# Borders between the 18 stages of two transformer stacks: sums signalled by quarters, squares by quarters, and a new order on VectorE and ScalarE

## The chip, the cores and the metric

The kernel runs on one core of a Trainium2 chip. The metric is the device time of one execution, in microseconds (us). TensorE does the matrix products, ScalarE (ACT) and VectorE (DVE) everything between them, GpSimd (POOL) a few column operations, and SyncE (SP) only issues the loads of the weight stream.

## The reference, cut to what matters

The program pushes 256 tokens of width 1024 through two stacks. What the change touches is not the layers but what stands between them: residual addition and root mean square normalization.

```python
# first stack, 2 layers ("plain" borders)
x = x + 0.5 * swiglu(rms_norm(x, ffn1_norm[l]), ffn1_w13[l], ffn1_w2[l])
h = rms_norm(x, mix_norm[l])
...                                   # three attentions and gates, merged
x = x + jnp.sum(gates * proj, axis=2) @ w_out[l]
x = x + 0.5 * swiglu(rms_norm(x, ffn2_norm[l]), ffn2_w13[l], ffn2_w2[l])
...
return rms_norm(x, final_norm)
# second stack, 4 layers ("post" borders: the update is normalized as well)
x = x + 0.5 * rms_norm_2(swiglu_2(rms_norm_2(x, g[0]), ...), g[1])
m = ...attention(rms_norm_2(x, g[2]), ...)
x = x + rms_norm_2(m, g[3])
x = x + 0.5 * rms_norm_2(swiglu_2(rms_norm_2(x, g[4]), ...), g[5])
```

Everything is float32. A product is made of three products of split operands (high part times high, high times low, low times high), so each weight block and each activation is split into a high part (a cast) and a low part (a subtraction).

## The kernel before, in words

The tokens lie in two token tiles of 128 (tt = 0, 1), the features in two halves of 512; one token tile by one half is called a quarter here. Each stage (an FFN or an attention) ends in a product whose four quarters fill four banks of the accumulator `acc`. A "between" phase then makes the next stage's input out of them. There are 19 such phases, called border 0 to 18 here:

- border 0 opens the program (no addition, one norm). Borders 1 and 4 (FFN to the three-way attention, "mix"), 2 and 5 (mix to FFN) and 3 (FFN to FFN) are plain: add, then norm.
- border 6 (FFN to FFN) lies between the stacks: add, final norm, norm of the next stage.
- borders 7 to 17 are post: norm of the update, add, norm of the next stage. 7, 10, 13 and 16 lead from an FFN to an attention, 8, 11, 14 and 17 from an attention to an FFN, 9, 12 and 15 from FFN to FFN.
- border 18 closes the program: norm of the update, add, store.

The work of a border, by engine and by line of the file:

- ScalarE squares each quarter with a sum along the row (`mean_square`, L780), first of the update or of the changed x (`first_statistics`), then, where there are two norms, of x after that (`last_statistics`). It copies the turned activations out of PSUM as high parts (`high_parts`, L810), and casts whole weight steps (`split`, L735).
- GpSimd turns a pair of sums into 1/rms (L697, then L700; `rstd_ready`).
- VectorE multiplies the update by its gain (`gained`, L1356), adds (`added`, L1365 plain or L1374 post), norms (`final_norm` L1385, `normed` L1395), makes low parts of the activations (`low_parts_of`, L1404) and of whole weight steps (`split`, L1298).
- TensorE fills a gap with a few transposes (`keep_busy`, L2060; 5 or 18 of them where the border is post or final, none where it is plain), turns the normed token tile (`arrive`, L2078), and begins the next stage's first product by token tiles (`lead_tokens`, L2105). Where the next stage is an FFN the lead is over two weight steps (`step` and `step + 1`), else over one.

All engines run in the written order, and wait on semaphores. The accumulator is announced by two signals: `acc_half` after both quarters of token tile 0, and the end of the last weight step (`step_used`) for token tile 1:

```python
def accumulated(eng, ph, tt):
    if tt == 0:
        eng.wait_ge(sem["acc_half"], base(ph, "acc_half"))
    else:
        eng.wait_ge(sem["step_used"], ph.step)
```

At the end of an FFN, TensorE runs over token tile, then weight step, then k, then half (`rows_by` does both halves, L2165 to L2167: three products of 512 columns for each k and half); at the end of an attention over token tile, then half. Each engine ends a phase with a drain and begins the next one by a wait for the other engines' phases (`enter`, L535). Weight steps are loaded into a ring of three; the load of step c + 3 waits until VectorE has made the low part of step c.

Of the kernel before, what the change touches and what calls it, by code (L numbers as in the profile page):

```python
# [275 lines left out]
def plan():  # L276
# [41 lines left out]
    def nsa():  # L318
# [8 lines left out]
                    cmp_pv=2, cmp_scored=1, cmp_added=8, acc_half=1))  # L327

    def mix(l):
# [9 lines left out]
                    uk_made=1, q_turned=1, gated=12, merged_ready=8, y_high=4, y_low=4, acc_half=1))  # L339

    def weave(kind, bias, bias0, groups, early, slots, sink=None):
# [8 lines left out]
                    lo_made=8, acc_half=1, keys_turned=int(kind == "gqa2")))  # L350
# [38 lines left out]
def transformer_stacks(nc, stream, prm_in, cst_in, fixed_bias, gains_in, x_in, out, limit=None):  # L389
# [14 lines left out]
    with ExitStack() as ctx:  # L404
# [118 lines left out]
        def enter(eng, me, ph):  # L523
# [37 lines left out]
        def accumulated(eng, ph, tt):  # L561

            if tt == 0:
                eng.wait_ge(sem["acc_half"], base(ph, "acc_half"))
# [163 lines left out]
        def _(act):  # L728
# [44 lines left out]
            def between(ph):  # L773
# [10 lines left out]
                def of_x(tt, n, change):  # L784

                    for half in range(2):
                        if changes:
                            act.wait_ge(sem["x_ready"],
                                        base(ph, "x_ready") + 2 * changes * tt + 2 * change - 1 + half)
                        mean_square(n, tt, half, x[:, tt, 512 * half:512 * half + 512])  # L790

                def first_statistics(tt):

                    if ph.after == "post":
                        accumulated(act, ph, tt)
                        for half in range(2):
                            mean_square(per_token * tt, tt, half, acc[:, 2 * tt + half, :])
                    else:
                        of_x(tt, per_token * tt, 1)

                def last_statistics(tt):

                    of_x(tt, per_token * tt + per_token - 1, changes)

                def high_parts(tt):

                    for half in range(2):
                        n, k0 = 2 * tt + half, 4 * half
                        act.wait_ge(sem["tposed"], base(ph, "tposed") + n + 1)
                        nc.scalar.copy(xhl[:, k0:k0 + 4, tt * P:(tt + 1) * P],  # L810
                                       ps[:, n, :].rearrange("p (k q) -> p k q", k=4)).then_inc(sem["hi_made"], 1)

                if not ph.pre:
                    for tt in range(TT):
                        first_statistics(tt)
                    return
                step = after_of(ph).step
                first_statistics(0)
                if per_token == 2:
                    last_statistics(0)  # L820
                    first_statistics(1)
                if ph.gains == 0:
                    split(0)
                if per_token == 1:
                    split(step + 1)
                high_parts(0)
                if per_token == 2:
                    last_statistics(1)
                    split(step + 1)
                    high_parts(1)  # L830
                    split(step + 2)
                else:
                    first_statistics(1)
                    split(step + 2)
                    high_parts(1)
# [455 lines left out]
        def _(dve):  # L1291
# [52 lines left out]
            def between(ph):  # L1344
# [6 lines left out]
                def gained(tt):  # L1351

                    dve.wait_ge(sem["gains_loaded"], b["gains_loaded"] + 16)
                    for half in range(2):
                        dve.wait_ge(sem["sq_ready"], b["sq_ready"] + 2 * per_token * tt + half + 1)
                        nc.vector.tensor_tensor(o[:, tt, columns_of(half)], acc[:, 2 * tt + half, :],  # L1356
                                                post[:, columns_of(half)], ALU.mult).then_inc(sem["y_ready"], 1)

                def added(tt):

                    if ph.after == "plain":
# [1631 lines left out]
```

## Time and profile before

| | us |
|---|---|
| three executions | 3355.66, 3356.3, 3361.0 (median 3356.3) |
| the profiled execution | 3355.69, its span 3353.9 |
| TensorE busy in it | 3273.1 (98%) |
| VectorE, ScalarE, GpSimd busy | 2032.9 (61%), 1741.4 (52%), 71.1 (2%) |
| granted TensorE clock, mean | 0.993 |

The span is what the trace covers; the execution's own time is 1.8 us longer. TensorE's busy time is modelled from starts, so products that overlap count once and short gaps inside a run of them don't show. A timeline row gives the start, the length, the engine, the line, the operation with its output and input, and how many were merged; in brackets stand the idle time before it and what ended it.

### The profile page before, as it was taken

What the parts mean: (1) busy time and instruction counts of PE and PEld (TensorE: products, weight loads), DVE (VectorE), ACT (ScalarE), POOL (GpSimd) and SP (SyncE); (2) the same over time, 40 slices, a digit from 0 to 9 for tenths busy, and PEclk for the clock granted to TensorE, in tenths of its full rate; (3) what the DMA queues carried; (4) which work ended last, traced back from release to release, by engine and by line L of the source; (5) the groups of instructions that cost most, each with busy time, mean ns of one, the idle gap of its engine ahead of it and who ended that gap; (6) DMA issues with size and microseconds to landing.
All of it is one profiled execution on the core that took longest, in us unless ns stands there. A gap on an engine that the chain in (4) does not pass through costs nothing.

```text
span 3353.9 us, 53172 instructions
## 1 busy us (share of the span) xinstructions
PE 3273.1 (98%) x20084; PEld 2897.6 (86%) x20084; DVE 2032.9 (61%) x2776; ACT 1741.4 (52%) x2538; POOL 71.1 (2%) x150
## 2 busy tenths in 40 slices
PE   7999999999999999999999999899999999999999
PEld 6899988888999888888888889788888988888887
DVE  5567565555675655557556566555656665656655
ACT  4457544444664444446545456444545654545644
POOL 0000000000000000000000000000000000000000
PEclk9999999999999999999999999899999999999999
DMA  6666445555644554545554555255455455555454
GB/s 246 219 226 217 148 176 188 188 188 188 220 174 144 180 188 176 189 174 176 200 187 177 188 185 186 82 200 188 180 187 197 164 182 187 184 187 191 160 189 174
DMA packets 105223, 618.85 MB, mean 185 GB/s; under 512 B 10833, under 2 KB 19153, under 8 KB 34801
## 3 DMA queue, kind: packets, MB, share of 16 engines
q1 hardware_dynamic: 84288, 562.07, 46.5%
q10 hardware_dynamic: 20784, 54.71, 4.9%
q8 instruction: 102, 1.67, 0.2%
q14 instruction: 49, 0.39, 0.0%
HBM read 615.62 MB, written 9.50 MB: 186 GB/s over the span
## 4 chain that ended last, share of the span: by engine, by line
PE 90%; DVE 4%; ACT 2%; issue 2%; POOL 1%; ACTq 0%; DMA 0%; POOLq 0%; DVEq 0%
PE ps L2031 24%; PE ps L2035 12%; PE ps L2166 7%; PE ps L2165 7%; PE ps L2167 7%; PE ps L2146 5%; PE ps L2148 5%; PE ps L2147 5%; PE ps L2105 3%; PE ps L2052 2%; PE ps L2054 2%; PE ps L2053 2%; ACT v L780 2%; DVE wlo L1298 1%; PE ps L2534 1%
## 5 line engine op out<-in xcount | busy, mean ns | idle before, releaser
L1298 DVE TENSOR_TENSOR wlo<-raw,whi 128x2048 fp32r<-128x2048 f32 x435 | 996.4, 2291 | 579.2 <-ACT whi L735 578.9
L2031 PE MATMUL ps<-xhl,whi 128*128 128x512 f32 x3456 | 1201.9, 396 | 0.0
L735 ACT CAST whi<-raw 128x2048 fp32r<-128x2048 f32 x435 | 827.7, 1903 | 145.4 <-PE ps L2167 111.1
L2035 PE MATMUL ps<-xhl,wlo 128*128 128x256 f32 x3456 | 893.1, 279 | 0.0
L2031 PEld LDWEIGHTS ps<-xhl,whi 128*128 128x128 f32 x3456 | 626.5, 188 | 121.8
L2035 PEld LDWEIGHTS ps<-xhl,wlo 128*128 128x128 f32 x3456 | 651.5, 189 | 37.5
L2166 PE MATMUL ps<-wlo,ht 128*128 128x512 f32 x1056 | 417.1, 395 | 0.0
L2165 PE MATMUL ps<-whi,ht 128*128 128x512 f32 x1056 | 417.1, 395 | 0.0
L2167 PE MATMUL ps<-whi,ht 128*128 128x512 f32 x1056 | 416.6, 394 | 0.0
L2146 PE MATMUL ps<-xhl,whi 128*128 128x256 f32 x1360 | 391.1, 288 | 1.6 <-DVE wlo L1298 1.6
L2148 PE MATMUL ps<-xhl,wlo 128*128 128x256 f32 x1360 | 385.4, 283 | 0.0
L2147 PE MATMUL ps<-xhl,whi 128*128 128x256 f32 x1360 | 385.3, 283 | 0.0
L1311 DVE TENSOR_TENSOR wlo<-raw,whi 128x512 fp32r<-128x512 f32 (+1 forms) x328 | 232.1, 745 | 72.8 <-ACT whi L744 69.9
L848 ACT COPY tg<-ps 128x512 f32<-128x512 f32 x108 | 63.4, 587 | 397.4 <-PE ps L2031 397.4
L2146 PEld LDWEIGHTS ps<-xhl,whi 128*128 128x128 f32 x1360 | 260.0, 191 | 4.1 <-DVE wlo L1298 2.4
L2147 PEld LDWEIGHTS ps<-xhl,whi 128*128 128x128 f32 x1360 | 259.9, 191 | 0.5
L2148 PEld LDWEIGHTS ps<-xhl,wlo 128*128 128x128 f32 x1360 | 259.7, 191 | 0.0
L2167 PEld LDWEIGHTS ps<-whi,ht 128*128 128x128 f32 x1056 | 198.2, 188 | 48.2
L2166 PEld LDWEIGHTS ps<-wlo,ht 128*128 128x128 f32 x1056 | 198.2, 188 | 47.6
L2165 PEld LDWEIGHTS ps<-whi,ht 128*128 128x128 f32 x1056 | 198.2, 188 | 43.1
L744 ACT CAST whi<-raw 128x512 fp32r<-128x512 f32 (+1 forms) x328 | 205.0, 669 | 13.6 <-PE ps L2148 8.9
L1459 DVE TENSOR_TENSOR g_sum<-ps,tg 128x512 f32<-128x512 f32 x108 | 74.6, 691 | 203.6 <-ACT tg L848 203.6
(308 smaller groups left out, 3869.9 us busy)
## 6 DMA issues: line engine op xcount, KB each, us to landing
raw<-stream SPq DMA_DIRECT2D x528, 1024.0 KB, 4.8
bias<-rel_bias ACTq DMA_DIRECT2D x80, 256.0 KB, 2.7
gain<-gains ACTq DMA_DIRECT2D x19, 1024.0 KB, 5.1
bias<-fixed_bias ACTq DMA_DIRECT2D x40, 256.0 KB, 2.8
rel_bias<-rel_vectors SPq DMA_DIRECT2D x16, 512.0 KB
x<-x_tokens ACTq DMA_DIRECT2D x1, 1024.0 KB, 5.0
y_tokens<-x ACTq DMA_DIRECT2D x1, 1024.0 KB, 3.9
s<-constants ACTq DMA_DIRECT2D x1, 512.0 KB, 6.4
```

What stands on the lines that cost most here:

```text
L735: nc.scalar.copy(whi[:, slot, :], raw[:, slot, :]).then_inc(sem["hi_ready"], 1)
L744: nc.scalar.copy(whi[:, slot, part], raw[:, slot, part]) .then_inc(sem["hi_ready" if piece == pieces - 1 else "hi_piece"], 1)
L1298: nc.vector.tensor_tensor(wlo[:, slot, :], raw[:, slot, :], whi[:, slot, :].bitcast(F32), ALU.subtract).then_inc(sem["lo_ready"], 1)
L1311: e = nc.vector.tensor_tensor(wlo[:, slot, part], raw[:, slot, part], whi[:, slot, part].bitcast(F32), ALU.subtract)
L2031: wide = lambda: pe.matmul(ps[:, bank, 0:2 * half], hi[:, k, col0:col0 + P], src[:, k0 + k, :], start=first and k == 0, stop=last and k == ...
L2035: e = pe.matmul(ps[:, bank, 0:half], lo[:, k, col0:col0 + P], src[:, k0 + k, 0:half], start=False, stop=False)
L2146: pe.matmul(dst, hi[:, k, col0:col0 + P], src[:, k, 0:T], start=k == 0, stop=False)
L2147: pe.matmul(dst, hi[:, k, col0:col0 + P], src[:, k, T:2 * T], start=False, stop=False)
L2148: e = pe.matmul(dst, lo[:, k, col0:col0 + P], src[:, k, 0:T], start=False, stop=k == n - 1)
L2165: pe.matmul(dst, hh, w[0][:, kk, cols], start=first and kk == 0, stop=False)
L2166: pe.matmul(dst, hh, w[1][:, kk, cols], start=False, stop=False)
L2167: e = pe.matmul(dst, hl, w[0][:, kk, cols], start=False, stop=last and kk == 1)
```

## The change

1. Four signals where there were two: `acc_half` is raised after each of the first three quarters, and `step_used` stands for the fourth. At the end of an FFN the loops over half and k change places in the last two steps, so that a quarter is finished before the next begins.
2. ScalarE no longer waits for VectorE's last phase when it enters a border (`enter`).
3. ScalarE squares each quarter on its own signal. In post borders the square of quarter (1, 0) waits until VectorE has multiplied that quarter by the gain (`y_ready`), and VectorE's multiplication of it waits for the sum's signal and not for the square: the two swap places on that quarter.
4. ScalarE's order in borders with one norm: the square of quarter (1, 0) goes ahead of the high parts of token tile 0, that of (1, 1) ahead of those of tile 1, and `split(step + 2)` behind the latter. In the others the order stays.
5. VectorE's order: `split(step + 1)` of borders with one norm goes from behind `normed(0)` to behind `normed(1)` (before an FFN) or behind the low parts of tile 1 (else). In border 6 the addition of token tile 1 goes ahead of `normed(0)`. In post borders the multiplication of quarter (1, 0) goes ahead of `normed(0)`, that of (1, 1) stays behind it.
6. TensorE turns token tile 1 before it waits for the high part of `step + 1` (`lead_tokens`).

```diff
-                    h_ready=n - 1, hh_ready=n - 1, ht_ready=n - 1, acc_half=1,
+                    h_ready=n - 1, hh_ready=n - 1, ht_ready=n - 1, acc_half=3,
...
-                if e == "pe" and ph.kind == "between":
+                if ph.kind == "between" and (e == "pe" or (me, e) == ("act", "dve")):
                     continue
...
-            if tt == 0:
-                eng.wait_ge(sem["acc_half"], base(ph, "acc_half"))
+            if (tt, half) != (1, 1):
+                eng.wait_ge(sem["acc_half"], base(ph, "acc_half") - 2 + 2 * tt + half)
...
+                def first_statistics(tt, half):
+
+                    if ph.after == "post":
+                        accumulated(act, ph, tt, half)
+                        if (tt, half) == (1, 0):
+                            act.wait_ge(sem["y_ready"], base(ph, "y_ready") + 3)
+                        mean_square(per_token * tt, tt, half, acc[:, 2 * tt + half, :])
+                    else:
+                        of_x(tt, half, per_token * tt, 1)
...
                 if per_token == 2:
                     last_statistics(0)
+                    first_statistics(1, 0)
+                    first_statistics(1, 1)
+                    high_part(0, 0)
+                    high_part(0, 1)
                     last_statistics(1)
                     split(step + 1)
+                    high_part(1, 0)
+                    high_part(1, 1)
                     split(step + 2)
                 else:
+                    if ph.gains == 0:
+                        split(0)
+                    split(step + 1)
+                    first_statistics(1, 0)
+                    high_part(0, 0)
+                    high_part(0, 1)
+                    first_statistics(1, 1)
+                    high_part(1, 0)
+                    high_part(1, 1)
                     split(step + 2)
...
-                    for half in range(2):
+                    if (tt, half) == (1, 0):
+                        accumulated(dve, ph, tt, half)
+                    else:
                         dve.wait_ge(sem["sq_ready"], b["sq_ready"] + 2 * per_token * tt + half + 1)
...
+                def changed(tt):
+
+                    if ph.after == "post":
+                        added(tt, 0)
+                        added(tt, 1)
+                    elif ph.after == "plain" and (tt == 0 or not ph.final):
+                        added(tt, 0)
+                        added(tt, 1)
+                    if ph.final:
+                        final_norm(tt)
...
+                changed(0)
                 if ph.after == "post":
-                    gained(0)
-                added(0)
+                    gained(1, 0)
                 if ph.final:
-                    final_norm(0)
+                    added(1, 0)
+                    added(1, 1)
                 normed(0)
+                if ph.after == "post":
+                    gained(1, 1)
                 pair_leads = after_of(ph).kind == "ffn"
...
+                if ph.gains == 0:
+                    split(0)
+                changed(1)
+                low_parts_of(0)
+                normed(1)
+                if pair_leads:
                     split(step + 1)
+                low_parts_of(1)
+                if not pair_leads:
+                    split(step + 1)
                 split(step + 2)
...
                 ends = (1, 0) if c == ph.step else (0, 1)
+                if between is not None:
+                    between()
                 high_made(c)
...
-                if between is not None:
-                    between()
                 products(0, 0, range(KD))
...
-                        for kk in range(2):
-                            e = rows_by(w, i, tt, kk, False, i == 1)
+                        for half in range(2):
+                            for kk in range(2):
+                                e = rows_by(w, i, tt, kk, half, False, i == 1)
+                            if i == 1 and (tt, half) != (1, 1):
+                                e.then_inc(sem["acc_half"], 1)
...
-                    if i == 3 and quarter == 1:
+                    if i == 3 and quarter < 3:
                         e.then_inc(sem["acc_half"], 1)
```

## Rows read from the trace of the kernel before

**Rows 1.** The page, the chain that ended last: share of the span by engine.

```profile
PE 90%; DVE 4%; ACT 2%; issue 2%; POOL 1%; ACTq 0%; DMA 0%; POOLq 0%; DVEq 0%
```

**Rows 2.** Waits of TensorE: line, releaser: us in total, times, longest us.

```profile
PE ps L2078 <- DVE o L1395: 22.3, 22, 7.5
PE ps L2105 <- DVE xhl L1404: 4.3, 13, 0.9
```

**Rows 3.** Timeline of border 7 (FFN to attention, post), TensorE, ScalarE, VectorE.

```profile
1495.11 0.39 PE L2165 MATMUL ps<-whi,ht 128*128 128x512 f32 x1
...
1500.47 0.40 PE L2167 MATMUL ps<-whi,ht 128*128 128x512 f32 x1
...
1501.95 1.32 PE L2078 MATMUL ps<-cst,o 128*128 128x128 f32 x8
...
1507.79 1.32 PE L2078 MATMUL ps<-cst,o 128*128 128x128 f32 x8 [0.72 <-DVE o L1395]
...
1495.39 0.60 ACT L780 ACTIVATE v<-ps 128x512 f32<-128x512 f32 x1 [2.52 <-PE ps L2167]
...
1502.65 1.25 ACT L810 CAST xhl<-ps 128x512 fp32r<-128x512 f32 x2 [0.47 <-PE ps L2078]
1504.45 0.63 ACT L780 ACTIVATE v<-x 128x512 f32<-128x512 f32 x1 [0.56 <-DVE x L1374]
...
1503.68 1.41 DVE L1374 SCALAR_TENSOR_TENSOR x<-o,small,x 128x512 f32<-128x512 f32 x2
```

**Rows 4.** Timeline of border 8 (attention to FFN, post), GpSimd and VectorE.

```profile
1588.67 0.30 POOL L697 TENSOR_SCALAR small<-small 128x1 f32<-128x1 f32 x1 [2.30 <-ACT v L780]
...
1589.82 0.81 POOL L697 TENSOR_SCALAR small<-small 128x1 f32<-128x1 f32 x1 [0.21 <-ACT v L780]
...
1589.72 1.42 DVE L1395 SCALAR_TENSOR_TENSOR o<-x,small,gain 128x512 f32<-128x512 f32 x2 [1.90 <-POOL small L700]
```

**Rows 5.** Timeline of border 1 (FFN to mix, plain), ScalarE, VectorE, TensorE.

```profile
213.01 1.07 ACT L810 CAST xhl<-ps 128x512 fp32r<-128x512 f32 x2 [1.83 <-PE ps L2078]
...
214.89 0.61 ACT L780 ACTIVATE v<-x 128x512 f32<-128x512 f32 x1
...
216.75 1.41 DVE L1395 SCALAR_TENSOR_TENSOR o<-x,small,gain 128x512 f32<-128x512 f32 x2 [0.73 <-POOL small L700]
218.87 1.36 DVE L1404 TENSOR_TENSOR xhl<-ps,xhl 128x512 fp32r<-128x512 f32 x2 [0.70 <-ACT xhl L810]
...
217.56 1.32 PE L2078 MATMUL ps<-cst,o 128*128 128x128 f32 x8 [0.70 <-DVE o L1395]
...
221.93 0.28 PE L2146 MATMUL ps<-xhl,whi 128*128 128x256 f32 x1
```

**Rows 6.** Timeline of border 2 (mix to FFN, plain) and the FFN's first steps.

```profile
473.96 2.28 DVE L1298 TENSOR_TENSOR wlo<-raw,whi 128x2048 fp32r<-128x2048 f32 x1
...
479.39 1.42 DVE L1395 SCALAR_TENSOR_TENSOR o<-x,small,gain 128x512 f32<-128x512 f32 x2 [0.75 <-POOL small L700]
...
491.50 0.42 DVE L1477 TENSOR_TENSOR h<-ps,silu 128x256 f32<-128x256 f32 x1
...
474.32 1.07 ACT L810 CAST xhl<-ps 128x512 fp32r<-128x512 f32 x2 [1.16 <-PE ps L2078]
...
477.51 0.61 ACT L780 ACTIVATE v<-x 128x512 f32<-128x512 f32 x1
...
492.80 0.60 PE L2203 MATMUL ps<-cst,h 128*128 128x128 f32 x4
```

**Rows 7.** Border 6 (between the stacks): timeline, and windows (PEclk third from the end).

```profile
1308.81 1.32 PE L2078 MATMUL ps<-cst,o 128*128 128x128 f32 x8 [0.95 <-DVE o L1395]
1311.99 1.19 PE L2105 MATMUL ps<-whi,xhl 128*128 128x256 f32 x4 [1.87 <-ACT xhl L810]
...
1313.32 0.63 ACT L780 ACTIVATE v<-x 128x512 f32<-128x512 f32 x1 [0.98 <-DVE x L1385]
...
1312.00:1313.00 1.00, 1.00 (x5) 1.00 (x6) 0.47 (x1) 0.34 (x1) 0.42 (x1) 0.50 0.00 0
```

More of the change, by code:

```diff
@@ L801, in last_statistics, with of_x @@
[L801 to L811, printed above, removed]
+                def of_x(tt, half, n, change):
+                    if changes:
+                        act.wait_ge(sem["x_ready"], base(ph, "x_ready") + 2 * changes * tt + 2 * change - 1 + half)
+                    mean_square(n, tt, half, x[:, tt, 512 * half:512 * half + 512])
@@ L813, in between, with high_part @@
+                def high_part(tt, half):
+                    n, k0 = 2 * tt + half, 4 * half
+                    act.wait_ge(sem["tposed"], base(ph, "tposed") + n + 1)
+                    nc.scalar.copy(xhl[:, k0:k0 + 4, tt * P:(tt + 1) * P],
+                                   ps[:, n, :].rearrange("p (k q) -> p k q", k=4)).then_inc(sem["hi_made"], 1)
+                first_statistics(0, 0)
+                first_statistics(0, 1)
                 if not ph.pre:
-                    for tt in range(TT):
-                        first_statistics(tt)
+                    first_statistics(1, 0)
+                    first_statistics(1, 1)
@@ L2157, in up, with rows_by @@
                     feature_tile(bank + 1, w, P, xhl).then_inc(sem["step_used"], 1)
-                def rows_by(w, buffer, tt, kk, first, last):
+                def rows_by(w, buffer, tt, kk, half, first, last):
                     hh, hl = (ht[:, buffer, kk, part, tt * P:(tt + 1) * P] for part in (0, 1))
-                    for half in range(2):
-                        cols = slice(512 * half, 512 * half + 512)
-                        dst = acc[:, 2 * tt + half, :]
-                        pe.matmul(dst, hh, w[0][:, kk, cols], start=first and kk == 0, stop=False)
-                        pe.matmul(dst, hh, w[1][:, kk, cols], start=False, stop=False)
-                        e = pe.matmul(dst, hl, w[0][:, kk, cols], start=False, stop=last and kk == 1)
-                    return e
+                    cols = slice(512 * half, 512 * half + 512)
+                    dst = acc[:, 2 * tt + half, :]
+                    pe.matmul(dst, hh, w[0][:, kk, cols], start=first and kk == 0, stop=False)
+                    pe.matmul(dst, hh, w[1][:, kk, cols], start=False, stop=False)
+                    return pe.matmul(dst, hl, w[0][:, kk, cols], start=False, stop=last and kk == 1)
                 def down(c, j=None, first=False):
@@ L2560, in out @@
                                    y_piece(i), part, first=i == 0, last=i == 3)
-                    if i == 3 and quarter == 1:
+                    if i == 3 and quarter < 3:
                         e.then_inc(sem["acc_half"], 1)
@@ L2710, in out @@
                                    br2[:, 2 * i:2 * i + 2, :], part, first=i == 0, last=i == 3)
-                    if i == 3 and quarter == 1:
+                    if i == 3 and quarter < 3:
                         e.then_inc(sem["acc_half"], 1)
```

98 lines of the change are left out of this document (29 added, 69 removed).

## The prediction, as written before the result was known

> **What bounds the kernel now.** I read the page first, and on it the chain that ended last: TensorE carries 90% of the span, VectorE, ScalarE, GpSimd and the issue of instructions about 9% together, some 300 us [rows 1]. The waits of TensorE say where such a share can become time: VectorE's norm, line L1395, is what the turning of the activations waits for, 22.3 us over 22 waits, and the low parts of the activations cost 4.3 us more [rows 2]. One of these waits, 7.5 us, is the start of the program, where the weights and constants land. So inside the stages TensorE never waits long, and what a change of the borders can win is bounded by these rows, to which come the moments in which the few filling transposes stand for work: some 25 us in all, of 3353.9. Then I read the timeline of one border of each kind, and looked in each for one thing: which instruction the turning of token tile 1 waits for, since tile 0 is done while TensorE still works on tile 1.
>
> **The post borders 7 to 17.** One quarter at the end of an FFN is six matmuls. The last 24 start from 1495.11 to 1500.47 [rows 3], 0.233 apart, so a quarter takes 1.40 and the accumulator is complete at 1500.47 + 0.40 = 1500.87. Before, ScalarE starts on both quarters of tile 0 at 1495.39, with 2.52 idle ahead. With its own signal the first quarter is squared 1.4 earlier, in that idle time, and the sum of tile 0 is complete one square (0.60) earlier. The same holds for tile 1: its first square goes ahead of the accumulator's end, and the second follows at 1500.9 and ends near 1501.5 instead of 1502.1.
>
> What does TensorE get of these 0.6? Tile 0: nothing. The turning starts at 1501.95 directly behind the filling transposes, with no wait in brackets, so it stays. The casts of its high parts therefore stay too, 1502.65 to 1503.90 [rows 3]. Tile 1: the second squares start at 1504.45 because VectorE's addition started at 1503.68, and 0.56 of ScalarE's idle time stands before them. In the new order the multiplication of quarter (1, 0) is done before the norm of tile 0, so the addition waits only for GpSimd and for one multiplication, and comes about 0.6 to 0.8 earlier; then ScalarE's casts, which end at 1503.90, are what is late next. So the second squares move by 1504.45 - 1503.90 = 0.55, and GpSimd, the norm and the turning at 1507.79 (with 0.72 of waiting before it) move along. Behind it the lead, the weight splits of VectorE and its end of phase all hang on the norm, and shift by the same. I take 0.55 for each of the eleven: **6.0 us**.
>
> The changed waits here: ScalarE's square of (1, 0) now waits for VectorE, which reaches that multiplication behind the addition of tile 0. Queued behind it are the second square, the casts and the second statistics, that is, all of the border. It costs nothing as long as that addition ends before 1499.5, when the third quarter's signal comes; before, the turning of tile 0 at 1501.95 already needed everything that follows from that addition, a square, GpSimd's two operations and a norm, about 3 us, so it does.
>
> GpSimd is the uncertain one. Its first operation took 0.30 when VectorE was idle, and 0.81 when it started 0.10 behind VectorE's norm [rows 4]. In the new order the first operation of tile 1 falls under that norm in every post border. If both operations lose 0.5 there, the addition comes only 0.3 earlier. So the bounds for a post border are 0.3 and 0.6, and I take the value that ScalarE's casts allow. The Trainium skill, SBUF — State Buffer, section "Who interferes with whom", has this as a rule: a VectorE instruction with two SBUF inputs and a GpSimd instruction that reads SBUF exclude each other, and the later one waits for the whole of the earlier; the norm reads x and the gain, both in SBUF. By that rule the wait would end with the norm's second half at the latest, and these borders would give between 3.3 and 6 us.
>
> **Border 18** has no second statistics; one square less on the last path, from [rows 3], and the multiplication is out of the way: **0.6 us**.
>
> **Border 6** has most to give. TensorE turns tile 0 at 1308.81 and then waits 1.87 for the casts, since ScalarE first squares tile 1, which VectorE adds only behind the norm of tile 0 [rows 7]. With the addition ahead of that norm, the squares are done when the turning is: casts 0.70 after it as in border 7 (1501.95 to 1502.65), from 1309.5 to 1310.75 by the length there [rows 3]. Then ScalarE takes the second squares of tile 1 at 1310.8 instead of 1313.32, if VectorE's final norm has made x by then; GpSimd under a norm makes that just so. This gives **2.5 us**. TensorE's clock stood at 0.50 of full in the microsecond behind the 1.87 of waiting [rows 7]; whether it does without that wait changes only how tight the lead is. Bounds 1.7 and 3.
>
> **Borders 2 and 5** (mix to FFN). VectorE's low part of `step + 1` (2.28) stands at 473.96, ahead of the addition of tile 1 [rows 6]. Without it, and with the second addition of tile 0 one half (0.65) earlier, because the first is done when its own signal comes, VectorE is at tile 1 by 473.3. ScalarE squares (1, 0) from 474.05 to 474.7; the casts, 1.07 long, now queue behind it and end at 475.8 rather than 475.4, which TensorE pays and gets back, since the low parts come early; the second square starts at 475.8 instead of 477.51. Norm and turning follow: 1.7. Late next is the FFN's first pair. The moved low part now lies between `normed(1)` at 477.7 (before, 479.39) and the low parts of tile 1, so VectorE's phase ends only 0.3 earlier, and with it come ScalarE's activation, the split of the next step, and VectorE's h, at 491.50 before and 491.2 now, 0.42 long. TensorE wants to turn the second tile of h 0.3 behind 492.80 - 1.7, at 491.4, and gets it at 491.6. So 0.2 goes back: 1.5 each, **3.0 us**, with bounds of 1.0 and 1.8.
>
> **Borders 3, 1 and 4** (from an FFN, plain). The casts stay behind TensorE, 213.01 to 214.08 [rows 5]; the second square follows at 214.08 instead of 214.89, since (1, 0) is squared ahead of the casts. The norm at 216.75 and the turning at 217.56, which waits 0.70 for it, move by 0.8. Border 3 keeps that: **0.8 us**. In 1 and 4 the low part of `step + 1` now comes behind the low parts of tile 1, which start at 218.87 and take 1.36. Moved by 0.8 they end at 219.4, the 2.28 [rows 6] end at 221.65, and the mix's second product, at 221.93 before, starts there: 0.3 each, **0.6 us**. Its load, that of `step + 4`, is issued that much later on SP's queue and has more than two weight steps of TensorE's work ahead of it. VectorE's phase ends about 1.4 later there, which ScalarE's entry into the mix waits for; TensorE's next want of it lies two products later. I take nothing for that, and 0.6 loss each as the other bound.
>
> **At nothing**: the two more signals (they ride on matmuls that are there); the change of loops in the FFN's last two steps (the same 48 matmuls, each with its own weights loaded before and after); the turning ahead of the wait for the high part (that cast ended before the turning in each border read; without that cover it would win some tenths); border 0, where the start of the constants' landing sets the pace (bounds: 0 and a loss of 0.3).
>
> **Sum**: 6.0 + 0.6 + 2.5 + 3.0 + 0.8 + 0.6 = 13.5 us. The profiled execution took 3355.69; 3355.69 - 13.5 = 3342.2, and on the median of the three runs, 0.6 above it, 3342.8.
>
> **The rivals.** (A) *GpSimd eats the post borders.* The lock of [rows 4] holds up both its operations, and these borders give 0 to 0.3 instead of 0.55: 3 to 6 us less, 3346 to 3349. For it speak the 0.81; against it that VectorE's multiplication, which follows the norm, takes one input from PSUM. (B) *Given back.* The turning comes earlier, but the next stage's start hangs on VectorE's end of phase and ScalarE's entry, as in border 2. If all borders into an FFN behind an attention (2, 5, 8, 11, 14, 17) and those into an attention (1, 4, 7, 10, 13, 16) lost their gain there, 3.0 + 0.6 + 8 x 0.55 = 8.0 would go, 5.5 us of gain stay: 3350.8, no change by the measure. Against it: in the post borders that end of phase moves along. (C) *Slower: the clock.* In border 6 the lead runs at 0.50 behind a wait for the casts. A matmul of 256 columns takes half of 0.233 [rows 3], the first sixteen of a lead 1.9, and at half clock 1.9 more. If the new order made the first casts late, so that TensorE fell to 0.50 there, each border would lose 1.9; from eight borders on that outweighs the sum, and with borders 1 to 17 the time is 3342.8 + 32 = 3375. For it: in borders 2 and 5 the casts come 0.4 later. Against it: the waits in the others read are 0.7 [rows 3, 5], the mean granted clock of 0.993 leaves no room for many such stretches now, and the waits shrink in sum. (D) *More*: the mix's second product doesn't wait, h is in time, and ScalarE starts nearer to the signals: 3 us more, 3339 to 3340.
>
> **How the numbers follow.** As summed, within 2.5 us: 0.55; A 0.20; B 0.10; C 0.05; D 0.10. The likeliest is the sum, 3342.8. The lower bounds add up to 11 x 0.3 + 0.4 + 1.7 + 2.0 + 0.6 - 1.2 - 0.3 = 6.5 us, hence 3349.8; the upper ones to D, with one microsecond of scatter 3338. The range is 3338 to 3349.8, which leaves out C, most of B and a part of D. A difference of 0.2%, 6.7 us, is about what a measurement of this kernel can tell from none. Faster by more than that (below 3349.6): the sum, A and D, and a little of B, 0.86; within it 0.09; slower 0.05.
>
> **What would show it.** Right: ScalarE's first square of a border begins 1.4 before the second; the turning of tile 1 in border 7 comes 6.4 behind the accumulator's end instead of 1507.79 - 1500.87 = 6.9; no wait of 1.87 in border 6; the waits of L2078 for L1395 fall from 22.3 to near 15. Wrong: GpSimd's L697 at 0.8 with the addition no earlier; TensorE waiting for L1298 at the mix's second product for more than 0.6; PEclk under 1.00 behind other borders than 6; ScalarE waiting at the square of (1, 0).

## The result, and the profile after

The changed kernel takes 3337.13 us (median of four runs, 3333.81 to 3337.63), the kernel before 3358.65 (four runs beside them, 3355.66 to 3361.09): a ratio of 0.9935, 95% interval 0.9923 to 0.9948, so 0.65% faster. The profiled executions stand at 3336.82 and 3355.69, 18.87 apart. The forecast was 3342.8 with a range from 3338. The direction is right, the gain between the profiled executions is 40% larger than the sum of 13.5 (between the medians it is 21.5), and the time lies just below the range.

The chain that ended last, on the page after, and TensorE's waits (line, releaser: us in total, times, longest), to be held against [rows 1, 2]:

```profile
PE 73%; PEld 15%; issue 4%; DVE 3%; ACT 2%; PEldq 2%; DMA 0%; POOLq 0%; DVEq 0%; POOL 0%; ACTq 0%
```

```profile
PE ps L2088 <- DVE o L1409: 15.0, 14, 7.5
...
PE ps L2115 <- ACT xhl L809: 5.7, 16, 0.5
...
PE ps L2156 <- DVE wlo L1303: 2.4, 6, 0.4
```

The turning (L2088, before L2078) waits 15.0 us for the norm, not 22.3, and 14 times instead of 22; the 13 waits of borders are together 7.5 us. The waits for the low parts of the activations, 4.3 before, are gone; the leads now wait 5.7 us for the casts of the activations, 16 times and never more than 0.5. In the chain VectorE is down from 4% to 3%, and GpSimd from 1% to none; what it lists as PEld are TensorE's weight loads, so TensorE carries 88% of it.

Border 7, timeline after (TensorE, ScalarE, VectorE, GpSimd), as [rows 3] before. A PEld row is the loading of a matmul's weights, which TensorE does for each transpose too:

```profile
1491.21 0.40 PE L2176 MATMUL ps<-whi,ht 128*128 128x512 f32 x1
1491.97 0.74 PE L2070 MATMUL ps<-cst 128*128 128x128 f32 x5 [0.37 <-PEq L535]
1492.44 0.91 PEld L2088 LDWEIGHTS ps<-cst,o 128*128 128x128 f32 x8
1492.55 1.04 PE L2088 MATMUL ps<-cst,o 128*128 128x128 f32 x8
...
1497.60 1.32 PE L2088 MATMUL ps<-cst,o 128*128 128x128 f32 x8 [0.58 <-DVE o L1409]
...
1484.73 0.60 ACT L780 ACTIVATE v<-ps 128x512 f32<-128x512 f32 x1 [1.12 <-PE ps L2176]
...
1486.05 0.60 ACT L780 ACTIVATE v<-ps 128x512 f32<-128x512 f32 x1 [0.63 <-PE ps L2176]
...
1491.10 0.60 ACT L780 ACTIVATE v<-ps 128x512 f32<-128x512 f32 x1 [1.02 <-DVE o L1363]
...
1493.18 1.07 ACT L809 CAST xhl<-ps 128x512 fp32r<-128x512 f32 x2 [0.82 <-PE ps L2088]
1494.27 0.63 ACT L780 ACTIVATE v<-x 128x512 f32<-128x512 f32 x1
...
1491.22 1.41 DVE L1409 SCALAR_TENSOR_TENSOR o<-x,small,gain 128x512 f32<-128x512 f32 x2 [0.22 <-POOL small L700]
...
1493.48 1.42 DVE L1377 SCALAR_TENSOR_TENSOR x<-o,small,x 128x512 f32<-128x512 f32 x2 [0.24 <-POOL small L700]
...
1492.46 0.34 POOL L697 TENSOR_SCALAR small<-small 128x1 f32<-128x1 f32 x1 [1.34 <-ACT v L780]
```

The accumulator is complete at 1491.21 + 0.40 = 1491.61. From there, with the kernel before in brackets (complete at 1500.87): tile 0 turned at +0.94 [+1.08], its two casts from +1.57 to +2.64 [+1.78 to +3.03], the second squares of tile 1 at +2.66 [+3.58], tile 1 turned at +5.99 [+6.92]. The squares now follow the casts with no idle time, as forecast; but the casts themselves end 0.39 earlier, which was not. One of the forecast's signs of being wrong is there as well: ScalarE waits 1.02 at the square of (1, 0) for VectorE's multiplication. It costs next to nothing here: the second square still starts at 1491.69, 0.08 behind the accumulator's end.

Border 6 after, timeline of TensorE and windows (PEclk third from the end), as [rows 7] before:

```profile
1302.12 1.32 PE L2088 MATMUL ps<-cst,o 128*128 128x128 f32 x8 [1.05 <-DVE o L1409]
1303.54 0.71 PE L2115 MATMUL ps<-whi,xhl 128*128 128x256 f32 x4
```

```profile
1304.00:1305.00 1.00, 1.00 (x11) 1.00 (x10) 1.00 (x3) 1.00 (x4) 0.00 (x0) 1.00 0.00 0
```

The first product follows the turning directly, where it waited 1.87, and the lead runs at a granted clock of 1.00.

Border by border, from the accumulator's end to the first matmul behind the lead (border 0: from its last matmul before the border), profile after less profile before, in us:

| borders | forecast | measured |
|---|---|---|
| 7, 9, 10, 12, 13, 15, 16 (behind an FFN) | -0.55 each | -0.92 or -0.93; 9: -1.30 |
| 8, 11, 14, 17 (behind an attention) | -0.55 each | -1.10, -1.03, -1.09, -1.09 |
| 7 to 17 together | -6.0 | -11.15 |
| 18 (to the end) | -0.6 | -0.54 |
| 6 | -2.5 | -2.56 |
| 2 and 5 | -1.5 each | -2.03 each |
| 3 | -0.8 | -0.89 |
| 1 and 4 | -0.3 each | -0.33, -0.35 |
| 0 | 0 | -1.25 |
| the stages between | 0 | +2.25 (attention between borders 10 and 11: +1.92) |

These sum to 18.87. Two lines of the table look like effects and turn out to be scatter: border 0 and the attention stage (below). And 0.37 of border 9's 1.30 belong to one late start in the profile before: VectorE's norm of tile 0 begins there 0.47 behind the end of GpSimd's second operation, in border 12 0.11. No run shows why.

### The profile page after: what moved, and what is told of

It reads as the page before. It is cut to its first block, busy times and chain, and to the rows that moved or that the text cites. A ratio compares the mean times of both kernels' runs of the same rounds, so it can differ in the third digit from the quotient of the medians.

```text
span 3335.0 us, 53201 instructions
## 1 busy us (share of the span) xinstructions
PE 3264.3 (98%) x20084; PEld 2898.0 (87%) x20084; DVE 2035.8 (61%) x2776; ACT 1742.0 (52%) x2538; POOL 69.5 (2%) x150
## 4 chain that ended last, share of the span: by engine, by line
PE 73%; PEld 15%; issue 4%; DVE 3%; ACT 2%; PEldq 2%; DMA 0%; POOLq 0%; DVEq 0%; POOL 0%; ACTq 0%
PE ps L2041 19%; PE ps L2045 10%; PE ps L2175 5%; PE ps L2174 5%; PE ps L2176 5%; PE ps L2156 4%; PE ps L2158 4%; PE ps L2157 4%; PE ps L2115 3%; PEld ps L2041 3%; PEld ps L2045 2%; PEldq L535 2%; PEld ps L2176 2%; PEld ps L2174 2%; PEld ps L2175 2%
## 5 line engine op out<-in xcount | busy, mean ns | idle before, releaser
L2156 PE MATMUL ps<-xhl,whi 128*128 128x256 f32 x1360 | 391.7, 288 | 2.4 <-DVE wlo L1303 2.4
L2156 PEld LDWEIGHTS ps<-xhl,whi 128*128 128x128 f32 x1360 | 260.3, 191 | 5.3 <-DVE wlo L1303 3.6
```

What stands on the lines that cost most here:

```text
L2156: pe.matmul(dst, hi[:, k, col0:col0 + P], src[:, k, 0:T], start=k == 0, stop=False)
```

## The experiments

All are edits of the changed kernel, and what they cost is read border by border against the profile after, where unedited borders from 1 on agree to 0.1 or better, mostly to 0.02. A loss is a longer border. Line numbers of the edited files shift by a few lines.

**E1. One signal for tile 0** (the post borders): ScalarE's first square waits for both quarters.

```diff
-    accumulated(act, ph, tt, half)
+    accumulated(act, ph, tt, 1 if tt == 0 else half)
```

> The changed kernel, but in the post borders ScalarE's first square of tile 0 waits for the second quarter's signal, as in the kernel before. The prediction held that tile 0 gives TensorE nothing, since the filling transposes fix the start of its turning: then borders 7 to 17 keep their length (0.0 each). The theory formed from the profile after is that VectorE's norm of tile 0 paced that turning in the kernel before, and that a chain on VectorE (norm of tile 0, multiplication of (1, 1), addition of tile 1) carries a delay of tile 0 on to tile 1: then the sum of tile 0 is 0.5 to 0.6 later, the addition of tile 1 is 0.4 to 0.55 later, and each of the eleven borders is 0.3 to 0.5 longer, 3 to 5 us in all. Border 18 may lose the same; the others nothing.

Measured: 0.33 in each border behind an FFN (0.32 to 0.34), 0.48 to 0.50 in each behind an attention; borders 7 to 17 lose 4.28 (3343.38 us). The turning of tile 0 goes back by the 0.14 and the first product by 0.20. Tile 0 is not worth nothing. Border 7 of this run, TensorE and VectorE:

```profile
1492.63 0.74 PE L2070 MATMUL ps<-cst 128*128 128x128 f32 x5 [0.36 <-PEq L535]
1493.35 0.42 PEld L2088 LDWEIGHTS ps<-cst,o 128*128 128x128 f32 x4 [0.22 <-DVE o L1409]
1493.35 1.32 PE L2088 MATMUL ps<-cst,o 128*128 128x128 f32 x8
...
1492.55 1.42 DVE L1409 SCALAR_TENSOR_TENSOR o<-x,small,gain 128x512 f32<-128x512 f32 x2 [0.88 <-POOL small L700]
```

From the first filling transpose to the turning it is 0.72, as before (1501.23 to 1501.95), against 0.58 after. The norm starts at 1492.55 and its first half is done 0.7 later, at about 1493.25: the turning has waited for it. The row of the matmuls brackets no wait, but that of their weight loads does, 0.22 for the norm (L1409). The second four transposes wait for the norm's second half, which stretches the turning from 1.04 to 1.32.

**E2. ScalarE waits for VectorE's end of phase** when it enters a border, as before.

```diff
-    if ph.kind == "between" and (e == "pe" or (me, e) == ("act", "dve")):
+    if e == "pe" and ph.kind == "between":
```

> The changed kernel, but ScalarE enters a border only when VectorE has left the stage before, as in the kernel before. In border 7 of the changed kernel VectorE's last low part of the FFN ends at 1485.93, and ScalarE's first square starts at 1484.73. So if tile 0 counts (theory from the profile after), the borders behind an FFN (7, 9, 10, 12, 13, 15, 16) lose 0.3 to 0.5 each, like with one signal for tile 0, and those behind an attention lose nothing, where VectorE is done early: 2 to 3.5 us. If tile 0 gives nothing (the prediction), no border changes. The plain borders lose nothing by either, since there ScalarE waits for VectorE's addition anyway.

Measured: 0.53 or 0.54 in all seven borders behind an FFN, 0.02 or less in those behind an attention (3.76 together; 3340.65 us). VectorE's last low part of the FFN ends after the first quarter's signal, so the quarter signal is of no use without the wait's removal: in this run the second square of tile 0 starts at 1486.73 on a border that is complete at 1491.69, 0.60 nearer to its end than after, as in E1. That it costs 0.20 more than E1 there is GpSimd's doing. Border 7 of this run, GpSimd and VectorE:

```profile
1492.55 0.86 POOL L697 TENSOR_SCALAR small<-small 128x1 f32<-128x1 f32 x1 [0.74 <-ACT v L780]
...
1491.91 1.41 DVE L1409 SCALAR_TENSOR_TENSOR o<-x,small,gain 128x512 f32<-128x512 f32 x2 [0.82 <-POOL small L700]
...
1494.09 1.41 DVE L1377 SCALAR_TENSOR_TENSOR x<-o,small,x 128x512 f32<-128x512 f32 x2 [0.16 <-POOL small L700]
```

The norm has moved onto GpSimd's first operation, which takes 0.86 instead of 0.34, and the addition waits for it.

**E3. The multiplication of (1, 0) behind the norm of tile 0**, together with that of (1, 1). ScalarE's square of (1, 0) no longer waits for it; VectorE waits for that square instead, as before. The order in the file:

```diff
     changed(0)
-    if ph.after == "post":
-        gained(1, 0)
     ...
     normed(0)
     if ph.after == "post":
+        gained(1, 0)
         gained(1, 1)
```

> The changed kernel, but VectorE multiplies quarter (1, 0) behind the norm of tile 0, with (1, 1), and ScalarE's square of (1, 0) doesn't wait for it, as in the kernel before. The prediction put the whole gain of a post border, 0.55, down to this order: then each of the eleven loses about 0.55, and what is left of its gain is what came on top. By the theory from the profile after this order is only one of two parts: VectorE ends the two multiplications 0.5 to 0.6 later than GpSimd is done, the addition's first half is late by 0.35 to 0.45 against ScalarE, and each border loses 0.35 to 0.45, 4 to 5 us in all, and the rest of the 0.92 to 1.10 measured belongs to tile 0.

Measured: 0.27 to 0.29 behind an FFN, 0.45 or 0.46 behind an attention, 3.78 together (3335.53 us in all, less than after; the attention stage below is why). The order that the forecast held for the whole cause gives 0.28 of 0.92 and 0.45 of 1.10 when undone by itself.

**E4. Fewer filling transposes**: 12 behind an attention in place of 18, none behind an FFN in place of 5.

```diff
-    keep_busy(18 if ... else 5 if ... else 0, 3)
+    keep_busy(12 if ... else 0, 3)
```

> The changed kernel with 12 filling transposes in place of 18 behind an attention, and none in place of 5 behind an FFN. If the casts of tile 0 are what the second squares of tile 1 wait for, as the prediction has it, the turning starts 0.5 to 0.6 earlier and each post border gains about 0.5: 5 us. If the addition of tile 1 comes next (in border 7 after, its first half ends at 1494.19, the casts at 1494.25), behind an FFN the gain is 0.05 or less, behind an attention 0.2 to 0.3 (addition's first half at 1581.75, casts to 1582.0): 1 us in all. A third: with fewer transposes TensorE's clock falls to half, and the leads of these borders take up to 1.9 more each.

Measured: tile 0 is turned 0.42 and 0.51 earlier, and of that the borders behind an FFN lose 0.02, those behind an attention gain 0.14 or 0.15; border 6, whose five fills are gone too, loses 0.24 (3333.88 us). Border 7 of this run, ScalarE, then border 6, TensorE and its window (PEclk third from the end):

```profile
1493.92 1.19 ACT L809 CAST xhl<-ps 128x512 fp32r<-128x512 f32 x2 [0.43 <-PE ps L2088]
1495.41 0.63 ACT L780 ACTIVATE v<-x 128x512 f32<-128x512 f32 x1 [0.30 <-DVE x L1377]
```

```profile
1303.12 1.59 PE L2088 MATMUL ps<-cst,o 128*128 128x128 f32 x8 [2.27 <-DVE o L1409]
```

```profile
1304.00:1305.00 1.00, 1.00 (x6) 0.50 0.00 0
```

The casts are done earlier, and the second squares now wait 0.30 for VectorE's addition. So behind an FFN casts and addition are even in the changed kernel, and earlier casts alone give nothing. The third thing expected came true in one border: the granted clock is 1.00 over the leads of all the post borders, but in border 6, where TensorE now idles 2.27 before the turning, it is 0.50 from 1304 until past 1307. With the fills that wait is 1.05 and the clock stays at 1.00.

**E5. The low part of the second weight step ahead of the addition of tile 1** (one-norm borders, 0 to 5), ScalarE's new order kept.

```diff
+    if per_token == 1:
+        split(step + 1)
     changed(1)
     low_parts_of(0)
     normed(1)
```

> The changed kernel, but in the borders with one norm (0 to 5) VectorE makes the low part of the second weight step (2.28 us) ahead of the addition of tile 1 again, while ScalarE keeps its new order (square of (1, 0) ahead of the casts). If VectorE's order carries these borders, the addition comes 2.28 later, the square and the casts queued behind it too, and TensorE's first product waits for them: 2, 3 and 5 lose 2.0 to 2.4 each, 1 and 4 about 1.6 (their low part is done early in exchange), 8 to 11 us in all, more than the change gave there. If ScalarE's order does the work and VectorE's addition has room, as the prediction's terms for 1, 3 and 4 have it (the squares wait for the casts), these lose nothing and 2 and 5 at most 1.7. Border 0: nothing if its 1.25 is the time at which TensorE starts to run at full pace, 0.9 to 1.25 if it is VectorE's order.

Measured: 2.76, 4.45, 3.09, 2.57 and 2.21 in borders 1 to 5 (3352.14 us), more than expected in four of five. That is 15.1 in sum, where the change gained 5.63: ScalarE's new order behind VectorE's old one is worse than either kernel, so this run shows that the new order needs the step moved, and not what the move gives by itself (E6 does). The turning of tile 1 is later by 1.3 to 2.3 more than the first product in borders 1 to 4, and in these the windows show half clock. Border 0 lost 1.36, which decides nothing (see its scatter below). First products of borders 2 and 5 of this run, and the windows of border 2 (TensorE, then PEclk):

```profile
479.93 1.20 PE L2117 MATMUL ps<-whi,xhl 128*128 128x256 f32 x4 [2.75 <-ACT xhl L809]
480.92 1.05 PE L2117 MATMUL ps<-wlo,xhl 128*128 128x256 f32 x4
...
1129.03 0.71 PE L2117 MATMUL ps<-whi,xhl 128*128 128x256 f32 x4 [2.75 <-ACT xhl L809]
1129.58 0.64 PE L2117 MATMUL ps<-wlo,xhl 128*128 128x256 f32 x4
```

```profile
477.00:478.00 1.00, 0.18 (x2) 1.00 0.00 0
478.00:479.00 1.00, 0.00 (x0) 0.89 0.00 0
479.00:480.00 1.00, 0.07 (x1) 0.50 0.67 98
...
485.00:486.00 1.00, 1.00 (x8) 0.70 0.00 0
```

The same wait of 2.75 leaves the lead of border 2 at a granted clock of 0.50 (1.2 GHz) until past 485, and that of border 5 at full clock.

**E6. ScalarE casts tile 0 before it squares tile 1** (one-norm borders).

```diff
-    first_statistics(1, 0)
     high_part(0, 0)
     high_part(0, 1)
+    first_statistics(1, 0)
     first_statistics(1, 1)
```

(and the split of the third step stands ahead of the casts of tile 1 again.)

> The changed kernel, but in the borders with one norm ScalarE casts tile 0 before it squares either quarter of tile 1, and splits the third step before the casts of tile 1, as before. If one square (0.63) then stands behind the casts that stood ahead of them, the norm of tile 1 comes 0.6 later and borders 1 to 5 lose 0.6 each, 3 us, while the first product of 2 and 5 comes 0.2 earlier. Rival: the order of VectorE alone gives the gain, and nothing is lost in 2 and 5, where ScalarE waited for the addition before.

Measured: 0.60 or 0.61 in 1, 3 and 4, 0.45 and 0.40 in 2 and 5, whose first product comes 0.18 and 0.21 earlier (3340.28 us). One square too many behind the casts costs its own length. The rival, that VectorE's order alone gives the gain, falls in 1, 3 and 4: 0.29 of 0.89 is left in border 3, and 1 and 4 lose more than the 0.33 and 0.35 that the change gave. In 2 and 5, 1.58 and 1.63 of 2.03 are left, so there VectorE's order, with the quarter signals (the two were not taken apart), gives most of it.

**E7. The addition of tile 1 in border 6 behind the norm of tile 0.**

```diff
     if ph.final:
-        added(1, 0)
-        added(1, 1)
```

(and `changed(1)` makes it.)

> The changed kernel, but in border 6 VectorE adds tile 1 behind the norm of tile 0 again. The prediction's step: the squares of tile 1 then stand ahead of the casts and wait for that addition, TensorE waits about 1.9 between the turning and its first product and falls to half clock behind it, and border 6 loses 2.5. If the new order only moves the wait, it loses less than 1. No other border changes. If the half clock alone makes up the loss, the first product comes as late as before (1.75) but the turning of tile 1 is later by less than that.

Measured: 2.61 in border 6, 0.02 in every other from 1 on (3338.97 us). TensorE and windows of border 6 in this run:

```profile
1306.27 0.71 PE L2112 MATMUL ps<-whi,xhl 128*128 128x256 f32 x4 [1.87 <-ACT xhl L809]
1306.82 0.64 PE L2112 MATMUL ps<-wlo,xhl 128*128 128x256 f32 x4
1307.29 0.77 PE L2112 MATMUL ps<-whi,xhl 128*128 128x256 f32 x4
1307.86 1.06 PE L2112 MATMUL ps<-wlo,xhl 128*128 128x256 f32 x4
```

```profile
1307.00:1308.00 1.00, 1.00 (x9) 1.00 (x9) 1.00 (x2) 0.40 (x1) 0.00 (x0) 0.82 0.00 0
```

The wait of 1.87 and the fall of the clock behind it are back. The first product is 1.77 later, the turning of tile 1 2.60.

**E8. E1, E2 and E3 together.**

> The three edits undone together for the post borders: one signal for tile 0, ScalarE's wait for VectorE's phase, the multiplication of (1, 0) behind the norm. If nothing else in the change touches these borders, the whole gain goes back: 0.92 in those behind an FFN and 1.10 in those behind an attention, 11 us in all. By simple addition of the parts measured one by one it is 0.81 (wait for the phase and order; the one signal is then covered by that wait) and 0.96. If the loops of the FFN's last steps or the turning ahead of the wait for the high part have a share, what is lost stays under 0.7.

Measured: 0.94 or 0.95 behind an FFN, 1.09 to 1.11 behind an attention, 11.03 in all (3348.95 us) against the 11.15 that the change gave. So these three edits are the whole gain of the post borders but for the 0.37 of border 9, and the new loops of the FFN's last steps, tile 1's own signal for its first quarter and the place of the turning have no share that shows by themselves.

**E9 and E10. Can the remaining wait be filled?** In the lead of an FFN the turning of tile 1 comes behind the eight products of the second step that need no low part of the weights:

```diff
-    if between is not None:
-        between()
     high_made(c)
     ...
     products(0, 0, range(KD))
+    if between is not None:
+        between()
     products(1, 0, range(KD))
```

with 12 fills behind an attention (E9); and in borders 8, 11, 14 and 17 ScalarE's split of that step ahead of the casts of tile 0 and VectorE's low part in two halves around the norm (E10).

> The changed kernel with the turning of tile 1 one product later in the lead of an FFN: TensorE first does the eight matmuls of the second weight step that need no low part of the weights, and turns then; and 12 filling transposes in place of 18 behind an attention. Of the 15.0 us that the turnings wait for VectorE's norm, 7.5 lie in borders 3 to 17. If that wait is all that bounds these borders, those into an FFN (6, 8, 9, 11, 12, 14, 15, 17) gain their wait, 0.4 to 0.7 each, some 4.5 us. If the low part of the second step, which the change put behind the norm of tile 1, is late next (in border 9 it ends at 1778.34 and TensorE wants it at 1778.59), each gains 0.25 and then waits there, with 0.14 more behind an attention: 2.5 us. If everything behind hangs on VectorE's end of phase, nothing. Against the changed kernel; against the kernel before 21 us more.

> The kernel of the last expectation, and in the post borders between an attention and an FFN (8, 11, 14, 17) ScalarE splits the second weight step ahead of the casts of tile 0, in 1.9 us of its idle time, so that VectorE can make one half of its low part ahead of the norm of tile 1 and the other behind it. If the low part was what was late, these four gain 0.4 to 0.7 each in place of 0.39. If ScalarE's split makes the casts late or VectorE's half the norm, they gain less than 0.39 or lose. The other borders as in the last kernel.

Measured: E9 3337.90 us (ratio to the kernel before 0.9946, 0.9929 to 0.9962), E10 3336.64 (0.9941, 0.9925 to 0.9958): both like the changed kernel, 0.9935. In E9 the borders into an FFN gain 0.09 to 0.12, behind an attention in the second stack 0.27 or 0.28, and the FFNs behind border 0 and behind the six borders that follow an attention give back 0.5 to 0.7 each. TensorE's waits in E9:

```profile
PE ps L2088 <- DVE o L1409: 10.8, 6, 7.4
...
PE ps L2115 <- ACT whi L735: 4.3, 8, 0.6
...
PE ps L2212 <- DVE h L1487: 2.3, 7, 0.5
```

Of 7.5 us of border waits for the norm 3.4 are left, but 4.3 have come for the high part of the second step, which ScalarE casts only behind the second squares, and 2.3 for h. None of the three waits expected was it, though the sum is that of the third, nothing: the low part was not the next thing late, the high part was. E10 takes the wait for the high part away in its four borders (1.9 over 4 waits remain, in the others), where the casts now come later, so that they gain only 0.16 to 0.19; h is waited for as often as in E9, 7 times. VectorE's h and what stands before it bound the start of these FFNs; a version faster than the changed one was not found. Outside border 0 and the attention stage told of below, the profile of E9 is 1.5 us longer than that of the changed kernel and that of E10 2.3; E10's lower median says nothing against it, since in its profile that stage alone is 5.4 shorter.

## Why the prediction was off, point by point

**Post borders 7 to 17: the failed step.** "Tile 0: nothing. The turning starts at 1501.95 directly behind the filling transposes, with no wait in brackets, so it stays", and with it the casts. This fixed the second squares of tile 1 at a gain of 0.55; they gained 0.92 in border 7 (+3.58 to +2.66). E1 and E8 show the turning 0.72 behind the first fill when the norm is late and 0.58 when it isn't: five fills take 0.58, and 0.14 was a wait for VectorE's norm, which the matmuls' row doesn't bracket. More than that start counted: the second four transposes wait for the norm's second half, and so did the second cast. With tile 0 early, the casts end 0.39 earlier in border 7, and of the 0.55 of ScalarE's idle time 0.02 is left: 0.39 + 0.53 make the 0.92. The rows that told it stood in the trace of before, in border 7 (TensorE, VectorE):

```profile
1501.23 0.74 PE L2060 MATMUL ps<-cst 128*128 128x128 f32 x5 [0.36 <-PEq L535]
...
1501.95 0.42 PEld L2078 LDWEIGHTS ps<-cst,o 128*128 128x128 f32 x4 [0.22 <-DVE o L1395]
1502.61 0.42 PEld L2078 LDWEIGHTS ps<-cst,o 128*128 128x128 f32 x4 [0.24 <-DVE o L1395]
...
1501.15 1.41 DVE L1395 SCALAR_TENSOR_TENSOR o<-x,small,gain 128x512 f32<-128x512 f32 x2 [1.90 <-POOL small L700]
```

The weight loads of the turning bracket what its matmuls don't: 0.22 for the norm's first half and 0.24 for its second; after, all eight follow the fills without a wait. The norm's two halves are done only at 1502.56, and casts of 1.25 rather than 1.07 [rows 3 against rows 5] are casts that wait between their halves. The bounds of 0.3 and 0.6 inherited the error, since both left tile 0 alone. Borders 1 to 18 gave 19.9 where the sum had 13.5; of the 6.4 that it fell short, 5.15 lie in this term (0.37 of them border 9's late norm) and 1.06 in borders 2 and 5.

One by one the three edits lose 4.28, 3.76 and 3.78, in sum 11.82; undone at once, 11.03. So with tile 1's order back (E3), the two edits of tile 0 still cost 11.03 - 3.78 = 7.25 more. Undone first, they cost about 5.7: E2 in the seven borders behind an FFN (there the squares of tile 0 start within 0.07 of where E1 has them) and E1 in the four behind an attention. So between 5.7 and 7.25 hang on tile 0, which the forecast had put at nothing, and 3.8 to 5.3 on tile 1, where it had 6.0.

**Rival A, GpSimd.** In border 7 after its first operation takes 0.34, since it starts 1.24 behind the norm. Behind an attention it does fall under the norm's first half:

```profile
1579.24 0.76 POOL L697 TENSOR_SCALAR small<-small 128x1 f32<-128x1 f32 x1 [0.26 <-ACT v L780]
1580.09 0.84 POOL L700 TENSOR_TENSOR small<-small 128x1 f32<-128x1 f32 x1
...
1579.09 1.42 DVE L1409 SCALAR_TENSOR_TENSOR o<-x,small,gain 128x512 f32<-128x512 f32 x2 [1.30 <-POOL small L700]
1580.43 0.68 DVE L1363 TENSOR_TENSOR o<-ps,gain 128x512 f32<-128x512 f32 x1
1581.03 1.40 DVE L1377 SCALAR_TENSOR_TENSOR x<-o,small,x 128x512 f32<-128x512 f32 x2
```

(border 8 after, GpSimd and VectorE). Both operations are stretched, 0.76 and 0.84 against 0.30 and 0.56, but they end at 1580.93, while VectorE is busy with norm and multiplication until 1581.03 and has to come first anyway: the lock is there and costs nothing, as it did cost 0.2 in E2. The Trainium skill, SBUF — State Buffer, section "Who interferes with whom", has the later of the two wait for the whole of the earlier; the trace agrees as far as it goes, since the first operation ends at 1580.00, behind the norm's first half.

**Borders 2 and 5**: 1.5 forecast, 2.03 measured. The order of things was right (VectorE's addition, square, casts, second square); the second square came 0.3 earlier than reckoned, as the casts took 0.94 from the first to the next square. The 0.2 given back did not occur: h was reckoned to come 0.3 earlier, and came 1.2 earlier, 17.03 behind the accumulator's end in border 2 and not 18.24. It is done at 489.20 and turned at 489.26 without a wait. **Border 6**, 2.5 and 2.56, with the fall of the clock gone as held possible. **Border 18**, 0.6 and 0.54; **3**, 0.8 and 0.89; **1 and 4**, 0.3 and 0.33 to 0.35, where the mix's second product waits for the low part that was moved, 2.4 us over 6 waits of L2156 in the whole program. E6 shows the 0.6 of one square behind casts at work in these.

**Rival B** did not happen in the changed kernel, but does in E9, with the h of the prediction's own reckoning as the place. **Rival C** did not: the granted clock is 1.00 from the turning to the end of the lead in every border after. Not because all the waits ahead of the leads shrank, as the prediction argued: that of border 6 did, from 1.87 to 0.10, but those of the post borders grew from 0.10 to 0.33 and those of 2 and 5 from 0.29 and 0.26 to 0.51 and 0.54. E5 shows that a wait of 2.75 can bring the half clock, and need not. **Rival D** came true in one of its three parts, h in time; the mix's second product does wait, and most of the surplus lies in tile 0 of the post borders, which D didn't name.

**Border 0** was put at nothing and reads 1.25. In the six of these runs that leave the orders of VectorE and TensorE there as in the changed kernel (E1 to E4, E7, E8) it is -0.14, 0.18, 0.26, 0.77, 0.88 and 1.25 longer than in the profile after. So the reading is within what one program shows from run to run, and no gain of the change is shown there. What moves is the time at which the first lead's matmuls of 256 columns go from 0.21 us each to 0.12: the eight that start at 26.00 take 1.91 before, those at 25.83 take 1.11 after, both at a recorded clock of 1.00.

**The attention between borders 10 and 11** took 1.92 longer after. Windows over that stage of before, after, E1 and E3 (TensorE busy, PEclk, DMA):

```profile
1983.94:2172.82 188.88, 173.35 (x1244) 0.90 0.44 152
```

```profile
1970.65:2161.45 190.80, 176.16 (x1244) 0.88 0.44 150
```

```profile
1972.80:2165.27 192.47, 177.77 (x1244) 0.88 0.43 149
```

```profile
1972.22:2157.65 185.43, 170.01 (x1244) 0.92 0.44 155
```

The same 1244 matmuls take 185.4 to 192.5 us in the profiled runs here, and the mean granted clock goes with it. Without this stage and border 0 the two profiles are 18.87 + 1.92 - 1.25 = 19.5 apart.

## What to carry to other kernels

A wait that the row of the matmuls doesn't bracket can still set a time: read the row of their weight loads too, and put the filler's own length beside the time it covers, and the producer's end beside the consumer's start, before calling a start fixed. An operation that comes in halves and takes longer than its two halves elsewhere (1.25 against 1.07) is waiting inside. Read a change of a few us stage by stage, since one stage here scatters by 7 us while most borders repeat to a few hundredths; and when a wait is filled, name the three next inputs of the same engine first: here, once the norm's wait was filled, high part and h were each late by up to half a us.

## What the runs showed of the hardware

The scatter of the whole time (3.8 us over four runs after, 5.4 before) has at least one place: one attention stage in which the granted clock falls to 0.50 for stretches whose place and length change from run to run (mean clock 0.88 to 0.92). And the same wait of TensorE, 2.75 us in E5, was followed by 0.50 in border 2 and by full clock in border 5, so that what a wait costs can be itself or nearly double: 2.21 and 4.45. The granted clock of 0.50 also followed waits of 1.87 (border 6, before and in E7), 2.20 (borders 1, 3 and 4 of E5) and 2.27 (border 6 of E4, without the fills), and none of the waits of up to 1.05 at borders 1 to 17 of the changed kernel. What decides between the two was not tried.
